# Masks of the products of keys ahead of the split of weights and of y's centring, and the blocks to invert loaded in two transfers

## The chip, the cores and the metric

One core of one Trainium2 chip. The metric is the device time of one execution in microseconds (us); lower is better. The core has TensorE (matrix products, in the rows PE; its weight loads PEld), VectorE (DVE), ScalarE (ACT), GpSimd (POOL) and SyncE (SP, which here issues every DMA). Each runs its own program in order and waits for the others by semaphores.

## The reference

One decoder block on x of 1024 positions by 2048 channels, in float32. A first RMSNorm, one input projection, and then two groups of heads side by side; their gated outputs go through one output projection, are added to x, and a last RMSNorm follows.

```python
h = rmsnorm(x, norm_gain[l])
proj = (h @ w_in[l]).astype(f32)
y_rwkv = rwkv7_group(...)            # 16 heads of 64 channels
y_attn = swa_sink_alibi_group(...)   # 16 query heads, 2 key/value heads, window of 128
x = x + concatenate([y_rwkv, y_attn]) @ w_out[l]
return rmsnorm(x, final_gain)
```

The first group (RWKV-7) is a recurrence over time for each head, `S = S * w + (-(S kk)) b^T + v k^T`, `y = S r`; then y is centred and scaled over the 64 channels of its head (`(y - mean) * rsqrt(var + eps)`), and gated. The second group is attention over a sliding window with a sink and linear position biases.

## The kernel before

**Tiling.** The sequence is taken in two halves of 512 positions, the heads in 8 pairs of 128 channels, so that there are 16 intervals of work, here called pairs 0 to 15 (`INTERVALS`; `i` in the helpers of the recurrence, and `j` in those of the channels). The projections run through everything as a background: weights come in quarters of a tile (128 x 512, 256 KB). For each quarter `gq` SyncE loads `w_raw` (`load_w`, L338), ScalarE rounds it to `w_hi` (`high`, L544), VectorE takes the rest `w_lo = w_raw - w_hi` (`low`, L749; its semaphore is `w_ready`), and TensorE makes 12 matmuls of 128 x 512 of it (`quarter`, L1179). There are 3 buffers of `w_raw` and 5 each of `w_hi` and `w_lo`.

**The order of the work.** All five engines walk over the same loop `for gq in range(QUARTERS)`. Each quarter of about 3 us is given, by hand, pieces of the pairs' work: `current(gq)` yields each pair j with its own quarter number `at = gq - base(j)`. A pair starts each 24 quarters (36 between pairs 7 and 8) and has 38 of them. So `at == 25` of pair j is the same quarter as `at == 1` of pair j + 1, in which `j - 1` stands for the pair whose recurrence is worked on. In each quarter, VectorE takes first `softmax_norm` (at 8), then `low(gq + 4)`, then some x tiles, then `masked` (at 1), then `recurrence` and `channels`, and last `centre` (at 24). ScalarE takes `high(gq + 4)` first. SyncE takes `load_w(gq + 6)` first, which waits for the split of the quarter three before it, since the buffer is shared:

```python
def load_w(gq):
    if gq >= RAW:
        sp.wait_ge(w_ready, gq - RAW + 1)
```

and then the transfers of `recurrence`: at 2 it waits for `a_read` (the masks) and stores four parts of the masked products in `scratch_L` (L378); at 3 it loads them back as `sub_l` (L385), spread over all 128 partitions; at 12 and 13 it brings the inverses back (L389 to L405). Then comes `load_up` (L369).

**The blocks to invert.** The recurrence needs, for each of 128 chunks, the inverse of a triangular matrix of keys. TensorE makes the products at 1 (`products`, L1243, in two halves, each ending in `a_full`); VectorE multiplies them by a mask into `am`, a part of `late` (`masked`, L919, four instructions, two for each half). GpSimd (`inverses`) turns the 32 x 32 diagonal blocks: in step s it reads row s of `sub_l`, in two instructions a step (L500, L502), 31 steps, and a copy (L503). After the way back over DRAM TensorE goes on at 16 with `under` (L1351), which waits for `x_back`.

**What else stands near.** After `products` TensorE makes the decay and learning-rate products of the next pair into banks 2 and 3 (L1205). ScalarE then takes at 26 the sigmoid of the last pair's gate (L619, which waits for `g_ready`, the end of the shift of g on VectorE, L782 and L783), and behind it at 2 the next pair's sigmoid of bank 2 (L596, semaphore `sigma_w`). TensorE's turns at 3 (`turns`, L1164) write bank 2 and wait for `sigma_w`. `centre` (L1025 to L1027) takes the mean out of y; ScalarE squares the result (L669). The sum of squares of r k (`rkr`) is split by L891 at 23 and used by TensorE at 24 (L1226). In the last pair of a half (`last_of_half`: 7 and 15) the tile GA_T is also read at 23.

Of the kernel before, what the change touches and what calls it, by code (L numbers as in the profile page):

```python
# [29 lines left out]
SUB = 32  # L30
SETS = 4
OWN = SUB // SETS
HALF = T // 2
SB = BT // 2
KEYS = BT + SB
# [123 lines left out]
def program(nc, io, scr):  # L159
    with ExitStack() as ctx:  # L160
# [8 lines left out]
        def sem(name):  # L169
# [113 lines left out]

        a_full, a_read = sem("a_full"), sem("a_read")
        t_full, t_read, kkt_full, kkt_read = sem("t_full"), sem("t_read"), sem("kkt_full"), sem("kkt_read")
        l_out, l_in, sub_done, x_out, x_back = (sem("l_out"), sem("l_in"), sem("sub_done"), sem("x_out"),
                                                sem("x_back"))
        s_full, s_read, negmax = sem("s_full"), sem("s_read"), sem("negmax")
        p_ready, p_norm = sem("p_ready"), sem("p_norm")
# [40 lines left out]
        with nc.Block() as block:  # L330
            @block.sync
            def _(sp):
# [38 lines left out]
                def recurrence(i, at):  # L371
                    if at == 2:
                        sp.wait_ge(a_read, 2 * i + 2)
                        blocks = scr["L"].rearrange("(x c m s t) -> x c s m t", x=2, c=2, s=SUB, t=SUB)
                        for x in range(2):
                            for c in range(2):
                                first = us_rows(c).start + SUB * x
                                sp.dma_start(blocks[x, c],  # L378
                                             am[first:first + SUB, :, :, c, 1 - c, SUB * x:SUB * (x + 1)].rearrange(
                                                 "s b h t -> s (b h) t")).then_inc(l_out, 16)  # L380
                    if at == 3:
                        sp.wait_ge(l_out, 4 * 16 * (i + 1))
                        sp.wait_ge(sub_done, i)
                        blocks = scr["L"].rearrange("(p f) -> p f", f=SUB * SUB).unsqueeze(1)
                        sp.dma_start(sub_l[:].rearrange("p s t -> p (s t)"),  # L385
                                     blocks.broadcast_to([PLACES, SETS, SUB * SUB])).then_inc(l_in, 16)
                    if at == 12:
                        sp.wait_ge(sub_done, i + 1)
                        sp.dma_start(scr["X"].rearrange("(p f) -> p f", p=HD), sub_io[0:HD, 0]).then_inc(x_out, 16)  # L389
                        rows = scr["XT"].rearrange("(p j q s) -> q p j s", j=OWN, q=SETS, s=SUB)  # L390
                        for q_ in range(SETS):
                            sp.dma_start(rows[q_], sub_xt[q_::SETS]).then_inc(x_out, 16)  # L392
                    if at == 13:
                        sp.wait_ge(x_out, (1 + SETS) * 16 * (i + 1))
                        columns = scr["X"].rearrange("(c m s j) -> c s m j", c=2, s=SUB, j=OWN)
                        for c in range(2):
                            first = us_rows(c).start
                            sp.dma_start(sub_io[first:first + SUB, 0].rearrange("s (m j) -> s m j", j=OWN), columns[c]
                                         ).then_inc(x_back, 16)
                        sp.wait_ge(u_full, 2 * i)  # L400
                        rows = scr["XT"].rearrange("(x m h t s) -> x h t m s", x=2, h=2, t=SUB, s=SUB)
                        for hh in range(2):
                            for x in range(2):
                                first = HD * hh + SUB * x
                                sp.dma_start(xt[first:first + SUB, :, SUB * x:SUB * (x + 1)], rows[x, hh]  # L405
                                             ).then_inc(x_back, 16)
                    h, n = divmod(i, PAIRS)
                    cols = slice(h * HALF, (h + 1) * HALF)
                    if at == 20:
                        sp.wait_ge(mixa_ready, 2 * i + 2)  # L410
                        sp.dma_start(scr["MIX"][PAIRS + n, :, cols], sa[:]).then_inc(mixa_stored, 16)
                    if at == 35:
                        sp.wait_ge(mix_ready, i + 1)
                        sp.dma_start(scr["MIX"][n, :, cols], ym[:].rearrange("p m t -> p (m t)")
                                     ).then_inc(mix_stored, 16)
# [64 lines left out]
            def _(pool):  # L480
# [7 lines left out]
                def inverses(i):  # L488
                    pool.wait_ge(x_out, (1 + SETS) * 16 * i)
                    if i:  # L490
                        pool.wait_ge(lev_full, 2 * i - 1)
                    pool.wait_ge(ident_landed, 16)
                    then(nc.gpsimd.tensor_copy(sub_io[:, 0], sub_ident[:]))
                    pool.wait_ge(l_in, 16 * (i + 1))
                    for s in range(SUB - 1):
                        below, width = SUB - 1 - s, s // SETS + 1
                        left = sub_l[:, s, s + 1:].unsqueeze(2).broadcast_to([P, below, width])
                        right = sub_x[:, s, 0:width].unsqueeze(1).broadcast_to([P, below, width])
                        t = sub_t[:, 0:below * width].rearrange("p (r c) -> p r c", c=width)
                        then(nc.gpsimd.tensor_tensor(t, left, right, ALU.mult))  # L500
                        rows = sub_x[:, s + 1:, 0:width]
                        then(nc.gpsimd.tensor_tensor(rows, rows, t, ALU.subtract))  # L502
                    then(nc.gpsimd.tensor_copy(sub_xt, sub_x.rearrange("p s j -> p j s")))  # L503
                    pool.sem_inc(sub_done, 1)
# [234 lines left out]
            def _(dve):  # L739
# [86 lines left out]
                def channels(j, at):  # L826
# [42 lines left out]
                    if at == (16 if last_of_half(j) else 20):  # L869
                        dve.wait_ge(kkt_full, j)  # L870
                        then(nc.vector.scalar_tensor_tensor(k, k, p(n, "k_k"), grow, ALU.mult, ALU.mult))
                        for c in range(2):
                            ins = nc.vector.tensor_tensor(
                                qr[:, :, 2 - c], k.rearrange(chunks, b=NB, c=2)[:, :, c],
                                decay[:, :, 0:C].rearrange("p (b c) t -> p b c t", c=2)[:, :, c], ALU.mult)
                        then(ins)
                        dve.sem_inc(kk_read, 1)
                    if at == (23 if last_of_half(j) else 16):
                        read_tile(tile_of(j, GA_T), g)
                        dve.sem_inc(ga_ready, 1)  # L880
# [5 lines left out]
                        evicted(tile_of(j, R_T), h, 4 * n + 2)  # L886
                    if at == (17 if last_of_half(j) else 20):
                        shift(r, p(n, "mu_r"))
                    if at == 23:
                        dve.wait_ge(rkr_high, j + 1)  # L890
                        then(nc.vector.tensor_tensor(kkt_r[:], s1, zs_r[:].bitcast(F32), ALU.subtract))  # L891
                        dve.sem_inc(rkr_split, 1)
                    if at == 19 and j % 4 == 0:
                        between_blocks(j)
                    if at == 21:
# [226 lines left out]
                for gq in range(QUARTERS):  # L1122
                    for j, at in current(gq):
                        if j >= 1 and at == 8:
                            softmax_norm(j - 1, 0)
                    if gq + 4 < QUARTERS:
                        low(gq + 4)
                    for j, at in current(gq):
                        if j >= 1 and at == 18:
                            keys_by_chunk(j - 1)  # L1130
                    cg = chunk_group(gq)
                    if cg:
                        slices(*cg)
                    for j, at in current(gq):
                        if j >= 1 and at == 1:
                            masked(j - 1, 0)
                            masked(j - 1, 1)
                    for j, at in current(gq):
                        if j >= 1:
                            recurrence(j - 1, at)  # L1140
                        if j < INTERVALS:
                            channels(j, at)
                    for j, at in current(gq):
                        if j >= 1 and at == 24:
                            centre(j - 1)
                    prepare(gq)
                    for u in range(2 * KC - 1):
                        if gq == done(OUT0 + u):
                            add(u)
                    if gq == 4 * OUT1 + 7:  # L1150
                        dve.wait_ge(fgain_landed, 16)
                        invert(0)
                    if 0 <= gq - 4 * OUT1 - 8 < KC:
                        scale(0, gq - 4 * OUT1 - 8)
# [400 lines left out]
```

## Time and profile before

| | |
|---|---|
| runs, median of 3 | 1896.99 us (1889.05 to 1900.61) |
| profiled execution | 1890.13 us, its span 1888.4 us |
| granted TensorE clock over the span | 0.993 of full speed (2.4 GHz) |
| TensorE, matmuls | 97% busy |
| VectorE | 66% busy |
| ScalarE | 42% busy |
| GpSimd | 25% busy |
| sixteen DMA engines, queue of SyncE | 36.7% of their time |

A share of busy time is an average over the whole span. TensorE's matmuls are pipelined, so a busy TensorE is not one at its peak, but its idle time is all that a reordering can give back. What a change is worth is read from the waits: who stood for whom, and how long. Times in the rows are microseconds from the start of the span, and `[1.01 <-DMA xt<-scratch_XT]` behind an instruction says that its engine stood idle for 1.01 us before it, until that transfer landed.

### The profile page before, as it was taken

The numbers are of one execution on the slowest core, as the hardware profiler recorded it, in microseconds if no ns is written. First come the engines' busy times: TensorE is split into PE (matmuls) and PEld (weight loads), VectorE is DVE, ScalarE is ACT, GpSimd is POOL, SyncE is SP. The second block draws the span as 40 slices with busy tenths as digits, with TensorE's granted clock in tenths as the row PEclk, the third lists the DMA queues.
The fourth block names the chain that finished last, engine by engine and source line by source line (L and its number), as shares of the span: only waits on it lengthen the run. The fifth ranks groups of instructions, "written<-read, shape, count | busy, mean of one in ns | idle before, by whom it ended". The sixth has DMA issues, their size and how long they took to land.

```text
span 1888.4 us, 38120 instructions
## 1 busy us (share of the span) xinstructions
PE 1840.0 (97%) x15008; PEld 1499.5 (79%) x15008; DVE 1245.9 (66%) x2255; ACT 788.2 (42%) x1578; POOL 466.3 (25%) x1096
## 2 busy tenths in 40 slices
PE   8999999999999999999999999999999999999996
PEld 5878878788888887888788878887877778888885
DVE  5676777677767677667677767676777754355333
ACT  6534444443434345444343434343534543242221
POOL 0005051423324150051423324150505060111110
PEclk9999999999999999999999999999999999999998
DMA  5533332333333336333333333333333543465443
GB/s 180 174 98 96 93 93 83 93 89 93 89 89 98 88 90 175 105 87 85 94 93 90 92 82 96 92 90 87 93 89 100 161 131 101 128 206 173 154 125 123
DMA packets 194962, 207.69 MB, mean 110 GB/s; under 512 B 98272, under 2 KB 101472, under 8 KB 194784
## 3 DMA queue, kind: packets, MB, share of 16 engines
q1 hardware_dynamic: 194784, 205.26, 36.7%
q8 instruction: 118, 1.93, 0.4%
q14 instruction: 60, 0.49, 0.1%
HBM read 183.18 MB, written 22.02 MB: 109 GB/s over the span
## 4 chain that ended last, share of the span: by engine, by line
PE 58%; POOL 16%; DVE 7%; DMA 7%; issue 5%; SPq 4%; ACT 1%; DVEq 0%; POOLq 0%; ACTq 0%
PE psum L1179 48%; POOL sub_io L502 8%; POOL sub_t L500 8%; DMA sub_l<-scratch_L 3%; DVE late L919 2%; DMA scratch_XT<-sub_io 1%; SPq L392 1%; PE psum L1308 1%; DMA xt<-scratch_XT 1%; SPq L405 1%; PE psum L1460 1%; PE psum L1424 1%; DVE w_lo L749 1%; DMA scratch_L<-late 1%; PE psum L1342 1%
## 5 line engine op out<-in xcount | busy, mean ns | idle before, releaser
L1179 PE MATMUL psum<-x_hi,w_hi 128*128 128x512 f32 x2144 | 873.4, 407 | 11.1 <-DVE x_lo L758 7.0
L1179 PE MATMUL psum<-x_hi,w_lo 128*128 128x512 f32 x2144 | 839.8, 392 | 0.0
L1179 PE MATMUL psum<-x_lo,w_hi 128*128 128x512 f32 x2144 | 838.9, 391 | 0.0
L749 DVE TENSOR_TENSOR w_lo<-w_raw,w_hi 128x512 fp32r<-128x512 f32 x536 | 372.0, 695 | 513.5 <-ACT w_hi L544 487.1
L544 ACT ACTIVATE w_hi<-w_raw 128x512 fp32r<-128x512 f32 x536 | 335.4, 629 | 780.8 <-PE psum L1179 685.9
L1179 PEld LDWEIGHTS psum<-x_hi,w_hi 128*128 128x128 f32 x2144 | 403.9, 188 | 111.0 <-issue 14.4
L1179 PEld LDWEIGHTS psum<-x_hi,w_lo 128*128 128x128 f32 x2144 | 403.8, 188 | 88.3
L1179 PEld LDWEIGHTS psum<-x_lo,w_hi 128*128 128x128 f32 x2144 | 404.8, 189 | 79.2 <-issue 3.9
L500 POOL TENSOR_TENSOR sub_t<-sub_l,sub_io 128x60 f32<-128x60 f32 (+24 forms) x496 | 188.3, 380 | 905.1 <-DMA sub_l<-scratch_L 867.4
L502 POOL TENSOR_TENSOR sub_io<-sub_io,sub_t 128x60 f32<-128x60 f32 (+24 forms) x496 | 199.5, 402 | 38.8
L521 POOL TENSOR_TENSOR v<-v,kb 128x512 f32<-128x512 f32 x29 | 38.3, 1321 | 269.1 <-ACT kb L693 268.7
L544 ACT ACTIVATE states<-psum,pc 128x64 f32<-128x64 f32 x112 | 35.0, 312 | 94.1 <-PE psum L1460 94.0
L544 ACT ACTIVATE late<-psum 64x256 f32<-64x256 f32 (+2 forms) x128 | 58.3, 482 | 17.0 <-PE psum L1342 16.3
L1460 PEld LDWEIGHTS psum<-states,score 128*128 128x128 f32 x256 | 47.9, 188 | 12.6 <-ACT states L544 2.0
L624 ACT ACTIVATE score<-score,top 128x192 f32<-128x192 f32 x128 | 56.3, 444 | 0.0
L868 DVE RECIPROCAL work<-work 128x512 f32<-128x512 f32 x16 | 53.6, 3353 | 2.0
L767 DVE TENSOR_TENSOR raw<-psum,rms 128x512 f32<-128x512 f32 x68 | 46.7, 686 | 3.4
L1308 PEld LDWEIGHTS psum<-pt,va 64*64 64x64 f32 (+1 forms) x512 | 34.9, 136 | 13.4 <-issue 11.3
L1460 PE MATMUL psum<-states,score 128*128 128x64 f32 x256 | 42.3, 246 | 0.7 <-ACT states L544 0.5
L919 DVE TENSOR_TENSOR late<-psum,cst 128x512 f32<-128x512 f32 x64 | 41.1, 683 | 2.7 <-DVE late L919 0.5
L1308 PE MATMUL psum<-pt,va 64*64 64x64 f32 (+1 forms) x512 | 41.5, 226 | 0.0
L1308 PE MATMUL psum<-pt,vs 64*64 64x64 f32 (+1 forms) x512 | 41.1, 226 | 0.0
(241 smaller groups left out, 1825.9 us busy)
## 6 DMA issues: line engine op xcount, KB each, us to landing
w_raw<-in_w_in SPq DMA_DIRECT2D x408, 256.0 KB, 2.6
w_raw<-in_w_out SPq DMA_DIRECT2D x128, 256.0 KB, 2.6
sub_l<-scratch_L SPq DMA_DIRECT2D x16, 512.0 KB, 4.7
stage<-in_x_t SPq DMA_DIRECT2D x20, 256.0 KB, 3.3
stage<-scratch_MIX SPq DMA_DIRECT2D x19, 256.0 KB, 4.0
late<-in_x_t SPq DMA_DIRECT2D x16, 256.0 KB, 3.0
scratch_MIX<-sa SPq DMA_DIRECT2D x16, 256.0 KB, 4.3
scratch_MIX<-ym SPq DMA_DIRECT2D x16, 256.0 KB, 3.2
```

The lines of the kernel that those rows point to most:

```text
L500: then(nc.gpsimd.tensor_tensor(t, left, right, ALU.mult))
L502: then(nc.gpsimd.tensor_tensor(rows, rows, t, ALU.subtract))
L521: then(nc.gpsimd.tensor_tensor(c_acc[:], c_acc[:], c_sq[u % 2], ALU.add))
L544: return nc.scalar.activation(dst, src, ACT.Copy, scale=scale)
L624: nc.scalar.activation(prob[:, x], prob[:, x], ACT.Exp, bias=top[:, 1, x:x + 1], accum_out=top[:, 2, x:x + 1])
L749: nc.vector.tensor_tensor(w_lo[gq % SPLIT][:], w_raw[gq % RAW][:], w_hi[gq % SPLIT][:].bitcast(F32), ALU.subtract).then_inc(w_ready, 1)
L767: then(nc.vector.tensor_tensor(dst, psum[:, s % 2], rms[s // H1][:], ALU.mult))
L868: then(nc.vector.reciprocal(grow, grow))
L919: ins = nc.vector.tensor_tensor(am[:, 2 * half:2 * half + 2, hh].rearrange("p b c x t -> p b (c x t)"), psum[:, bank].rearrange("p (b t) - ...
L1179: mm = nc.tensor.matmul(psum[:, s % 2], wt[gq % SPLIT][:, cols], xx[:, c], start=(c == 0 and wt is w_hi and xx is x_hi), stop=(c == KC - 1 ...
L1308: mm = nc.tensor.matmul(psum[head_rows(hh), (6, 2)[rnd], at:at + SB], keys, pt[keys_rows[f][hh], bb, f * P + sub * SB:f * P + (sub + 1) * SB],
L1460: nc.tensor.matmul(psum[:, 6, m * HD:(m + 1) * HD], mt[:, m], states[:, m], start=False, stop=True, skip_group_check=True).then_inc(state_ ...
```

## The change

VectorE's order in a quarter: `masked` (at 1) comes ahead of `low(gq + 4)`. `centre` moves from the end of quarter 24 to quarter 25, which is the same quarter as the next pair's `masked`, behind it and ahead of `low`. The split of rkr (L891) moves, within `channels`, ahead of the read of GA_T. The load of `sub_l` becomes two transfers: rows 0 to 7 of all blocks (128 KB), then rows 8 to 31 (384 KB), each with its own semaphore, and GpSimd waits for the second ahead of step 8. The programs of TensorE and ScalarE are unchanged, and so is all of SyncE's but the one load.

```diff
+ROWS = 8
@@ SyncE, at 3
-                        blocks = scr["L"].rearrange("(p f) -> p f", f=SUB * SUB).unsqueeze(1)
-                        sp.dma_start(sub_l[:].rearrange("p s t -> p (s t)"),
-                                     blocks.broadcast_to([PLACES, SETS, SUB * SUB])).then_inc(l_in, 16)
+                        blocks = scr["L"].rearrange("(p s t) -> p s t", s=SUB, t=SUB)
+                        for rows, landed in ((slice(0, ROWS), l_first), (slice(ROWS, SUB), l_rest)):
+                            part_ = blocks[:, rows].rearrange("p s t -> p (s t)").unsqueeze(1)
+                            sp.dma_start(sub_l[:, rows].rearrange("p s t -> p (s t)"),
+                                         part_.broadcast_to([PLACES, SETS, part_.shape[2]])).then_inc(landed, 16)
@@ GpSimd, inverses
-                    pool.wait_ge(l_in, 16 * (i + 1))
+                    pool.wait_ge(l_first, 16 * (i + 1))
                     for s in range(SUB - 1):
+                        if s == ROWS:
+                            pool.wait_ge(l_rest, 16 * (i + 1))
@@ VectorE, channels
+                    if at == 23:
+                        dve.wait_ge(rkr_high, j + 1)
+                        then(nc.vector.tensor_tensor(kkt_r[:], s1, zs_r[:].bitcast(F32), ALU.subtract))
+                        dve.sem_inc(rkr_split, 1)
                     if at == (23 if last_of_half(j) else 16):
                         read_tile(tile_of(j, GA_T), g)
                         dve.sem_inc(ga_ready, 1)
...
-                    if at == 23:
-                        dve.wait_ge(rkr_high, j + 1)
-                        then(nc.vector.tensor_tensor(kkt_r[:], s1, zs_r[:].bitcast(F32), ALU.subtract))
-                        dve.sem_inc(rkr_split, 1)
@@ VectorE, the loop over quarters
                         if j >= 1 and at == 8:
                             softmax_norm(j - 1, 0)
+                    for j, at in current(gq):
+                        if j >= 1 and at == 1:
+                            masked(j - 1, 0)
+                            masked(j - 1, 1)
+                    for j, at in current(gq):
+                        if j >= 1 and at == 25:
+                            centre(j - 1)
                     if gq + 4 < QUARTERS:
                         low(gq + 4)
...
-                    for j, at in current(gq):
-                        if j >= 1 and at == 1:
-                            masked(j - 1, 0)
-                            masked(j - 1, 1)
                     for j, at in current(gq):
                         if j >= 1:
                             recurrence(j - 1, at)
                         if j < INTERVALS:
                             channels(j, at)
-                    for j, at in current(gq):
-                        if j >= 1 and at == 24:
-                            centre(j - 1)
```

## Rows read from the trace of the kernel before

**Rows 1.** The page, part 1: engine, busy us (share of the span) x instructions.

```profile
PE 1840.0 (97%) x15008; PEld 1499.5 (79%) x15008; DVE 1245.9 (66%) x2255; ACT 788.2 (42%) x1578; POOL 466.3 (25%) x1096
```

**Rows 2.** Waits of TensorE, whole span: total us, times, longest us.

```profile
PE psum L1351 <- DMA xt<-scratch_XT: 15.4, 13, 2.6
...
PE psum L1226 <- DVEq L892: 4.4, 3, 4.0
```

**Rows 3.** Timeline of TensorE: first and last of 13 stops at L1351.

```profile
275.53 0.39 PE L1351 MATMUL psum<-sub_io,late 32*32 32x32 f32 x13 [1.01 <-DMA xt<-scratch_XT]
...
1552.15 0.36 PE L1351 MATMUL psum<-sub_io,late 32*32 32x32 f32 x12 [2.59 <-DMA xt<-scratch_XT]
```

**Rows 4.** Chain that ended last, pair 3: start, us, what.

```profile
405.98 1.64 DMA scratch_L<-late
407.64 4.64 DMA sub_l<-scratch_L
...
419.67 0.31 POOL sub_t L500
...
441.46 0.67 POOL sub_io L503
```

**Rows 5.** Timeline of all engines, pair 3: start, us, engine, line, instruction.

```profile
399.28 2.06 PE L1243 MATMUL psum<-qr,kb 64*128 64x128 f32 x32
...
399.46 0.68 DVE L1025 TENSOR_REDUCE stat<-ym 128x8 f32<-128x512 f32 x1
...
401.22 0.69 DVE L749 TENSOR_TENSOR w_lo<-w_raw,w_hi 128x512 fp32r<-128x512 f32 x1
401.82 2.72 DVE L919 TENSOR_TENSOR late<-psum,cst 128x512 f32<-128x512 f32 x4
401.93 0.33 SPq L338 DMA_DIRECT2D w_raw<-in_w_in  x1
404.63 1.81 SPq L378 DMA_DIRECT2D scratch_L<-late  x4
404.69 0.69 DVE L782 TENSOR_TENSOR work<-raw 128x512 f32<-128x512 f32 x1
405.42 0.75 DVE L783 SCALAR_TENSOR_TENSOR work<-work,par,raw 128x512 f32<-128x512 f32 x1
406.26 0.63 ACT L619 ACTIVATE work<-work 128x512 f32<-128x512 f32 x1 [0.37 <-DVEq L908]
...
406.80 0.67 ACT L596 ACTIVATE work<-psum,par 128x512 f32<-128x512 f32 x1
...
407.72 1.03 PE L1164 MATMUL psum<-cst,kb 128*128 128x128 f32 x8
```

**Rows 6.** Timeline, pair 0: the turns wait for ScalarE.

```profile
143.33 0.67 ACT L596 ACTIVATE work<-psum,par 128x512 f32<-128x512 f32 x1
...
144.14 0.52 PE L1164 MATMUL psum<-cst,kb 128*128 128x128 f32 x3 [0.67 <-ACT work L596]
```

**Rows 7.** Timeline, pair 3: VectorE's first softmax, and TensorE's use of it.

```profile
426.11 1.17 DVE L958 TENSOR_SCALAR score<-score,part 128x192 f32<-128x192 f32 x4
...
428.01 0.82 PE L1164 MATMUL psum<-cst,score 128*128 128x128 f32 x6
```

**Rows 8.** DMA issues: count, KB each, median us from issue to landing.

```profile
w_raw<-in_w_in SPq DMA_DIRECT2D x408, 256.0 KB, 2.6
...
lora_up<-in_lora_up SPq DMA_DIRECT2D x16, 64.0 KB, 4.1
...
sub_ident<-in_sub_ident SPq DMA_DIRECT2D x1, 128.0 KB, 2.3
```

**Rows 9.** The line L385 (`sub_l`), all 16 of its transfers.

```profile
DMA to landing us min/median/max: 3.8/4.7/5.3
```

**Rows 10.** Timeline of VectorE, pair 15, whose products start at 1497.96.

```profile
1500.82 0.69 DVE L1025 TENSOR_REDUCE stat<-ym 128x8 f32<-128x512 f32 x1
...
1508.48 0.69 DVE L749 TENSOR_TENSOR w_lo<-w_raw,w_hi 128x512 fp32r<-128x512 f32 x1
```

More of the change, by code:

```diff
@@ L285, in program @@
         t_full, t_read, kkt_full, kkt_read = sem("t_full"), sem("t_read"), sem("kkt_full"), sem("kkt_read")
-        l_out, l_in, sub_done, x_out, x_back = (sem("l_out"), sem("l_in"), sem("sub_done"), sem("x_out"),
+        l_out, l_first, l_rest, sub_done, x_out, x_back = (sem("l_out"), sem("l_first"), sem("l_rest"), sem("sub_done"), sem("x_out"),
                                                 sem("x_back"))
```

## The prediction

> **What bounds the kernel now.** I read the page first. TensorE is busy 97% of the span [rows 1], so the most that any reordering can give back is its idle time. The waits of TensorE tell where that is [rows 2]: 15.4 us in 13 stops at the first matmul of L1351 (`under`), which waits for the transfer that brings the inverted blocks home; 4.4 us at L1226, of which 4.0 us is one stop; and 0.67 us in one pair at L1164, for ScalarE's L596 [rows 6]. Nothing else that this change touches is of size. The 13 stops at L1351 (first and last in [rows 3]; in the order of the pairs they are 1.01, 1.44, 0.45, 0.86, 0.69, 0.70, then 1.26, 2.34, 0.36, 1.13, 0.74, 1.78, 2.59 us, for pairs 1 to 6, 8, and 10 to 15) are small beside the chain that ends in them. The chain of waits of one pair [rows 4] goes: masks on VectorE, four stores of blocks to DRAM whose last lands 1.64 us after its issue, the load of `sub_l` (4.64 us, to 412.28), GpSimd until 442.13 (some 30 us), and the way back. Its length from the products' first matmul to L1351 is fixed, so a chain that is shorter by d gives each pair the smaller of d and its stop, and a chain that is longer by d costs d.
>
> The timeline around the products [rows 5] shows the place of the edit. The products (L1243) run from 399.28 to 401.34. VectorE is behind at that moment and does centre (L1025, from 399.46), the split `low` (L749, 401.22 to 401.91), then four masks (L919, 401.82 to 404.54), then the shift of g (L782, L783, to 406.17). The other engines hang on it without slack: SyncE issues one weight load (L338) at 401.93, that is 0.02 us after the split, then the stores (L378) at 404.63, 0.09 us after the masks; ScalarE starts the sigmoid of g (L619) 0.09 us after the shift, then L596, which ends at 407.47; and TensorE starts the turns (L1164), which wait for L596, at 407.72.
>
> **The masks, moved ahead of centre and split.** Their work is unchanged. They can't start at 399.46, since they need the first half of the products. That half is done in the middle of L1243, about 400.37 (estimate: half of 2.06 us). So they run from about 400.45 to 403.17 (2.72 us), 1.37 us sooner than now; VectorE idles almost 1 us ahead of them, which it doesn't now. Centre then starts at 403.32 (a drain of 0.15 us, as between masks and L782), the split 1.76 us later (as 399.46 to 401.22) at 405.08, ending at 405.77 instead of 401.91.
>
> What queues behind the split? In SyncE's program, the quarter with the stores begins with `load_w(gq + 6)`, which waits for `w_ready` of gq + 4, the very split that is now behind masks and centre. SyncE is in order. So the weight load goes out at 405.79, takes 0.33 us to issue, and the stores begin at about 406.17: not 1.37 us sooner but 1.54 us later than 404.63. The early masks buy nothing on this chain, and the chain pays 1.54 us. The weight load itself, 3.9 us late, I cost at nothing: in the loops it is issued two quarters ahead of ScalarE's use of it, and lands 2.6 us after its issue [rows 8]. If that cover were gone, its 3.9 us would stand in the way of a quarter, in 13 pairs.
>
> **ScalarE and the turns.** The shift of g starts 0.60 us after the split's start (as L919 does now), at 405.68, and ends 1.48 us later at 407.16. L619 starts at 407.25, L596 0.54 us later at 407.79, and ends at 408.46. The pair in which the turns now stop longest for L596 shows the latency [rows 6]: L596 ends at 144.00, the matmul starts at 144.14. So the turns start at 408.60 instead of 407.72: TensorE stands for 0.88 us, a new stop in each of the pairs that have centre beside masks and a next pair's sigmoid, which are 13 (1 to 6 and 8 to 14). Behind it, ScalarE's evictions and exponentials come about 1 us late, and so does VectorE's first softmax; its last multiply ends at 427.28 now, and the matmul that needs it starts at 428.01 [rows 7]. With TensorE itself 0.88 us later, the slack of 0.73 us becomes 1.6 us, more than 1 us of delay: nothing added.
>
> A stop at the turns delays TensorE, not GpSimd, and so is paid out of the stop at L1351 where that one is longer.
>
> **The load of sub_l in two parts.** Now it lands 3.8 to 5.3 us after issue, 4.7 us at the median [rows 9]. GpSimd needs only the first 8 rows, 128 KB, to start. Bounds: nothing gained (the first part lands at 4.7 us too, because it queues behind the weight load, as a 64 KB load of `lora_up` issued right behind `sub_l` takes 4.1 us [rows 8]); and 3.1 us gained (it lands in the 1.6 us of a 32 KB store). I take the one row of 128 KB, `sub_ident`, 2.3 us: gained 2.4 us. The weight load ahead takes 2.6 us and will be issued about 1.1 us ahead, so it is mostly past. The second part is issued some 0.55 us later; GpSimd reaches step 8 at 419.67, 7.4 us after it could begin [rows 4], so its wait at step 8 is covered; without that cover it would cost what the part is late. One more issue on SyncE, 0.5 us, delays only `load_up`.
>
> The Trainium skill (DMA: Bandwidth & Descriptors, Anatomy of one DMA — SWDGE (gpsimd) path) gives a transfer about 2.0 us fixed and bytes over 436 GB/s, and so an estimate of 2.3 us for 128 KB and 3.2 us for 512 KB. By it the split would gain only 0.9 us, and the sum would be 7.5 us slower. The trace agrees with it on 128 KB (2.3 us) and not on 512 KB (4.7 us).
>
> **The split of rkr (L891) ahead of the read of GA_T.** It changes order only in pairs 7 and 15 (`last_of_half`). L1226 stops for it there for 0.17 and 0.16 us, which can't give more than 0.3 us. The large stop of 4.0 us is in pair 0, where nothing moves.
>
> **The sum.** Chain: 1.54 − 2.4 = −0.86 us. TensorE's own way: +0.88 us. A pair changes by the larger of (0.88 − its stop) and −0.86: for pairs 1 to 6 −0.13, −0.56, +0.43, +0.02, +0.19, +0.18; for 8 to 14 −0.38, +0.88 (pair 9 has no stop), −0.86, +0.52, −0.25, +0.14, −0.86. Together −0.7 us. Pair 15 is apart [rows 10]: VectorE reaches centre at 1500.82, 2.9 us after its products' start, so the masks lose nothing waiting; no sigmoid of a next pair follows; and the load of `sub_l` already waits for a later split (L749, 1508.48 to 1509.17), which moves by some 0.1 us. It gives 2.3 us of its 2.59. Pairs 0 and 7 have no stop and nothing to lose. With 0.3 us for rkr: −3.3 us. The profiled execution took 1890.1 us, so 1886.8; it lies 6.9 us below the median of the runs shown, 1897.0, and on that median the forecast is 1893.7.
>
> **Rivals.**
> A, the stops go away: if the turns don't stop anew (the new order lets ScalarE keep its time), each pair gives the smaller of 0.86 and its stop, 9.0 us, with pair 15 and rkr 11.6 us: 1885.4. If SyncE isn't held either, all of 15.4 + 0.3 us: 1881.3. For it speaks that the masks are ready sooner; against it L338 at 401.93 and L596's 0.25 us of slack. Chance 0.13.
> B, slower: the first part lands hardly sooner, and the late stores decide. It decides from a gain of under 1.55 us; with none, 13 pairs × 1.54 us − 0.3 = +19.8 us: 1916.8. For it speaks the `lora_up` row; against it `sub_ident`. Chance 0.10.
> B2, the transfer is mostly fixed cost, and a quarter of the bytes saves only 0.9 us (3.8 us, the shortest landing of `sub_l`): the chain is 0.64 us longer, twelve pairs × 0.64 + 0.88 − 0.8 (pair 15) − 0.3 = +7.5 us: 1904.5. Chance 0.09, as the median of 4.7 us speaks against so small a part for bytes. The rule of the Trainium skill above (DMA: Bandwidth & Descriptors) is of this kind.
> C, ScalarE's delay is handed on to the softmax or the evictions, and TensorE stops once more, 0.5 us in each of 13 pairs: up to +6.5 − 3.3 = +3.2 us, 1900.2. Against it the slack in [rows 7]. Chance 0.10.
> The forecast itself, −9 to +3 us, has 0.58.
>
> **How the numbers follow.** About 1% (19 us) is what a measurement of this kernel can tell from no change. Faster by more than that would need more than all stops at L1351: 0.04. Slower by more needs B with almost no gain, or B with C: 0.09. The rest, 0.87. The three runs before lie between 1889 and 1901, so the median of few runs is uncertain by some 5 us; with A on one side and B2 on the other, 1884 to 1906. The likeliest case's own range is 1889 to 1898.
>
> **What would show it.** VectorE idle ahead of L919 until the products are done, about 0.9 us in 13 pairs; L378 about 6.9 us after the start of L1243 (now 5.35); L619 about 8.0 us after it (now 6.98); a wait of TensorE at L1164 for L596 of about 11 us in total; L1351's waits down from 15.4 us to about 1 us; `sub_l`'s first part landing in 2.3 us; GpSimd's first multiply about 12.3 us after L1243 (now 13.1). If L378 stands at 4.0, SyncE's hold was misread; if GpSimd starts later than now, B; if L1164 shows no wait, A. Wrong would be above all a clearly shorter or longer first landing, since each 0.5 us of it moves seven or more pairs.

## Result: 0.37% slower

| | median | lowest to highest | runs |
|---|---|---|---|
| before | 1892.78 us | 1888.41 to 1902.30 | 20 |
| changed | 1899.87 us | 1895.48 to 1907.11 | 20 |

The ratio is 1.0037, with an interval of 1.0025 to 1.0049: 7.1 us slower, where 3.3 us faster was forecast. Measured again later (the last experiment below) it was 1.0036 (1.0022 to 1.0051).

Line numbers in the changed kernel are 1 to 5 higher: 339 for the weight load, 379 for the stores, 388 for `sub_l`, 505 and 507 for GpSimd's steps, 601 and 624 for the sigmoids, 754 for the split, 836 for VectorE's scan (831 before), 924 for the masks, 1030 for centre, 1169 for the turns, 1248 for the products, 1356 for `under`.

The waits of TensorE in the changed kernel (total us, times, longest us), which answer to [rows 2]:

```profile
PE psum L1169 <- ACT work L601: 10.8, 15, 0.8
PE psum L1356 <- DMA xt<-scratch_XT: 9.9, 12, 1.8
...
PE psum L1231 <- DVEq L886: 4.0, 1, 4.0
PE psum L1368 <- DVEq L1000: 1.6, 2, 1.2
...
PE psum L1248 <- DVEq L1066: 0.9, 1, 0.9
```

The new stop at the turns is there, 10.8 us. But the stops at `under` fell only from 15.4 to 9.9 us: the chain behind them did not get shorter.

The timeline of pair 3, which answers to [rows 5]; its products start at 400.02:

```profile
400.02 2.06 PE L1248 MATMUL psum<-qr,kb 64*128 64x128 f32 x32
...
401.23 2.72 DVE L924 TENSOR_TENSOR late<-psum,cst 128x512 f32<-128x512 f32 x4 [0.94 <-PE psum L1248]
...
404.10 0.69 DVE L1030 TENSOR_REDUCE stat<-ym 128x8 f32<-128x512 f32 x1
...
405.86 0.69 DVE L754 TENSOR_TENSOR w_lo<-w_raw,w_hi 128x512 fp32r<-128x512 f32 x1
...
406.58 0.33 SPq L339 DMA_DIRECT2D w_raw<-in_w_in  x1
406.95 1.92 SPq L379 DMA_DIRECT2D scratch_L<-late  x4
...
408.03 0.63 ACT L624 ACTIVATE work<-work 128x512 f32<-128x512 f32 x1 [1.07 <-DVEq L913]
...
408.57 0.67 ACT L601 ACTIVATE work<-psum,par 128x512 f32<-128x512 f32 x1
...
409.38 1.06 PE L1169 MATMUL psum<-cst,kb 128*128 128x128 f32 x8 [0.77 <-ACT work L601]
```

The masks wait 0.94 us for the products. The split ends at 406.55, the weight load goes out 0.03 us later and the stores behind it, 6.93 us after the products' start (5.35 before), though the masks were done at 403.95, which is 3.93 us after it. The sigmoid of g starts at 8.01 us (6.98 before), and the turns stop for 0.77 us.

### The profile page after: what moved, and what is told of

Its sections match the earlier page's. It is cut to its first block, busy times and chain, and to the rows that moved or that the text cites. A ratio compares the mean times of both kernels' runs of the same rounds, so it can differ in the third digit from the quotient of the medians.

```text
span 1900.8 us, 38152 instructions
## 1 busy us (share of the span) xinstructions
PE 1844.7 (97%) x15008; PEld 1500.5 (79%) x15008; DVE 1246.7 (66%) x2255; ACT 785.8 (41%) x1578; POOL 474.0 (25%) x1096
## 4 chain that ended last, share of the span: by engine, by line
PE 61%; POOL 17%; DVE 7%; DMA 6%; SPq 4%; issue 4%; ACT 1%; DVEq 0%; POOLq 0%; ACTq 0%
PE psum L1184 49%; POOL sub_io L507 8%; POOL sub_t L505 8%; DVE late L924 2%; DMA sub_l<-scratch_L 2%; PE psum L1313 1%; SPq L395 1%; DMA scratch_XT<-sub_io 1%; PE psum L1465 1%; DMA scratch_L<-late 1%; DMA xt<-scratch_XT 1%; SPq L408 1%; PE psum L1248 1%; PE psum L1429 1%; DVE w_lo L754 1%
## 5 line engine op out<-in xcount | busy, mean ns | idle before, releaser
L674 ACT ACTIVATE zs<-ym 128x512 f32<-128x512 f32 x16 | 10.1, 633 | 77.6 <-DVEq L1034 77.6
```

## What GpSimd meets when it begins

All distances below are in us from the start of a pair's products (only the fifth column is a length), averaged over the 13 pairs of the forecast (1 to 6 and 8 to 14), each read from the timeline of one profiled execution.

| run | stores | load of sub_l | GpSimd starts | its steps and copy | ends | `under` starts |
|---|---|---|---|---|---|---|
| before | 5.37 | 8.40 | 13.13 | 30.03 | 43.16 | 53.13 |
| changed | 6.93 | 10.18 | 13.02 | 30.69 | 43.71 | 53.69 |
| two loads only | 5.38 | 8.39 | 11.64 | 30.97 | 42.61 | 52.70 |
| moves only | 6.94 | 10.20 | 14.30 | 29.93 | 44.23 | 54.29 |
| centring back | 5.90 | 9.19 | 11.99 | 30.58 | 42.57 | 52.62 |
| stores first | 4.02 | 7.03 | 10.08 | 31.14 | 41.22 | 53.02 |
| both | 4.75 | 7.76 | 10.62 | 30.66 | 41.28 | 52.06 |
| scan first | 6.94 | 10.20 | 13.03 | 29.33 | 42.36 | 53.01 |
| two loads, scan first | 5.38 | 8.39 | 11.76 | 29.66 | 41.42 | 52.12 |

The chain to `under` grew by 0.56 us in the changed kernel, instead of shrinking by 0.86 us. One part of that is in the column that the forecast took as fixed: GpSimd's own time. Its first instructions in pair 1 of the kernel before, with VectorE's scan ahead of them (start us, us):

```profile
234.46 1.23 DVE L831 TENSOR_TENSOR_SCAN work<-keep,work 128x512 f32<-128x512 uint8 x1
```

```profile
235.78 0.24 POOL L500 TENSOR_TENSOR sub_t<-sub_l,sub_io 128x31 f32<-128x31 f32 x1 [47.26 <-DMA sub_l<-scratch_L]
236.10 0.28 POOL L502 TENSOR_TENSOR sub_io<-sub_io,sub_t 128x31 f32<-128x31 f32 x1
```

The same in the changed kernel:

```profile
235.78 1.26 DVE L836 TENSOR_TENSOR_SCAN work<-keep,work 128x512 f32<-128x512 uint8 x1
```

```profile
235.73 0.24 POOL L505 TENSOR_TENSOR sub_t<-sub_l,sub_io 128x31 f32<-128x31 f32 x1 [46.86 <-DMA sub_l<-scratch_L]
236.04 1.07 POOL L507 TENSOR_TENSOR sub_io<-sub_io,sub_t 128x31 f32<-128x31 f32 x1
```

Before, the scan ended at 235.69, just ahead of GpSimd. The shift of ScalarE's work that the forecast put at about 1 us carries the scan with it (it waits for `sigma_w`, and behind a scaling of y that waits for ScalarE too), and now it runs from 235.78 to 237.04. GpSimd's second instruction takes 1.07 us for what took 0.28 us, and ends at 237.11, with the scan (in pairs 3, 6, 10 and 11 its first instruction is caught instead, with 0.83 to 1.24 us for 0.24 us). GpSimd can start sooner, but it doesn't get on.

## Experiments

The theory after the result had four parts: (1) SyncE's weight load, behind the split, holds the stores; (2) centre ahead of the split makes the stop at the turns; (3) the first part of `sub_l` saves less than 2.4 us; (4) GpSimd doesn't proceed beside VectorE's scan. The rivals were that the two transfers bring nothing, that the turns alone cost the time, and that the second transfer, landing beside GpSimd's first steps, slows them.

**Two loads only.** The kernel before with the load in two parts.

```diff
-                        sp.dma_start(sub_l[:].rearrange("p s t -> p (s t)"),
-                                     blocks.broadcast_to([PLACES, SETS, SUB * SUB])).then_inc(l_in, 16)
+                        for rows, landed in ((slice(0, ROWS), l_first), (slice(ROWS, SUB), l_rest)):
...
+                        if s == ROWS:
+                            pool.wait_ge(l_rest, 16 * (i + 1))
```

> The kernel before, with the load of sub_l in two parts and nothing else changed. Theory: the changed kernel gains at this place what it loses at two others (SyncE's hold, the turns). Alone, the split starts GpSimd about 1.9 us sooner, 11.2 us after the products' start instead of 13.1, with no new stop at the turns; the 13 stops of L1351 (15.4 us) shrink to under 2 us and the kernel is 12 to 14 us faster (ratio about 0.993). GpSimd's inverses took 30.6 us in the changed kernel and 29.9 before: if the second transfer that lands beside them is the cause, they take 30.6 us here too, and the gain is nearer 11 us. Rival: two transfers cost as much as they bring, GpSimd starts at 12.5 us or later and the kernel is within 0.2% of before.

Measured: 1884.12 us against 1894.37 us of the kernel before, ratio 0.9945 (0.9925 to 0.9966), 10 us faster. GpSimd starts 1.5 us sooner, but its steps and copy take 0.9 us longer, so that it ends 0.55 us sooner on average, and 7.1 us of stops stay at `under`. In eleven of the 13 pairs it ended between 42.55 and 42.58 us, whether it had started at 11.21 or at 11.89 us. What holds it, in pair 1:

```profile
235.29 0.69 DVE L1075 TENSOR_TENSOR ym<-ym,stat 128x512 f32<-128x512 f32 x1
...
236.13 1.23 DVE L836 TENSOR_TENSOR_SCAN work<-keep,work 128x512 f32<-128x512 uint8 x1
```

```profile
235.29 0.79 POOL L505 TENSOR_TENSOR sub_t<-sub_l,sub_io 128x31 f32<-128x31 f32 x1 [45.10 <-DMA sub_l<-scratch_L]
236.16 1.26 POOL L507 TENSOR_TENSOR sub_io<-sub_io,sub_t 128x31 f32<-128x31 f32 x1
```

The split of the load is worth having; most of what it brings is then waited off behind the scan. The scan isn't alone in this: the scaling of y ahead of it (L1075, which has two inputs in SBUF too) held GpSimd's first instruction for 0.79 us instead of 0.24 us. The first expectation, 12 to 14 us, was too high, as were the stops that it left (under 2 us), and its second reading (30.6 us because of the second transfer, 11 us) had the right size: the next two runs tell which of the two causes is at work.

**Moves only.** The changed kernel with `sub_l` in one transfer again.

> The changed kernel with sub_l loaded in one transfer again; masks, centre and rkr stay moved. Theory (SyncE's weight load, queued ahead of the stores, waits for the split that is now behind masks and centre): stores at 6.9 us after the products' start, GpSimd starts at 14.6 to 15 us, TensorE stops 0.77 us at the turns in 13 pairs and the rest at L1356; 20 to 24 us slower than before (ratio about 1.011). If GpSimd's inverses take 30.6 us here, it is VectorE's new order that slows them, and the loss is nearer 28 us. Rival (the stores' time doesn't matter, the turns alone cost): 8 to 10 us slower, as the changed kernel.

Measured: 1911.04 us, ratio 1.009 (1.0069 to 1.011), 16.7 us slower. The stores stand at 6.94 us, so (1) holds without the split, and the rival of the turns alone (8 to 10 us) falls. GpSimd takes 29.93 us: VectorE's order does not slow it by itself, since at 14.30 us it starts behind the scan. GpSimd starts 4.1 us after the load's issue instead of 4.7 us, and the loss was under the 20 us expected. What changed around the load is that the weight load now goes 2.0 us ahead of it, where it went 0.6 us ahead before; that this is the cause was not tested by itself. The kernel before, pair 3:

```profile
407.03 0.35 SPq L338 DMA_DIRECT2D w_raw<-in_w_in  x1
407.64 0.54 SPq L385 DMA_DIRECT2D sub_l<-scratch_L  x1
```

The run with the moves only, the same pair:

```profile
409.07 1.91 SPq L379 DMA_DIRECT2D scratch_L<-late  x4
411.02 0.46 SPq L339 DMA_DIRECT2D w_raw<-in_w_in  x1
413.00 0.54 SPq L386 DMA_DIRECT2D sub_l<-scratch_L  x1
```

**Centring back.** The changed kernel with `centre` at the end of quarter 24.

```diff
-                        if j >= 1 and at == 25:
-                            centre(j - 1)
...
+                        if j >= 1 and at == 24:
+                            centre(j - 1)
```

> The changed kernel with y's centring back at the end of quarter 24; masks still ahead of the weight split. Theory: VectorE then does centre while the products are made, masks from 1.9 to 4.7 us, the split to 5.5 us, the stores go out at 5.9 us (6.9 in the changed kernel, 5.35 before), the shift of g ends as before and the stop at the turns is gone (10.8 us to under 1 us). Together with the two loads GpSimd starts about 12 us after the products; 8 to 10 us faster than before (ratio about 0.995). Rival (masks ahead of the split are what costs at the turns, not centre): 0.7 us stops at the turns stay.

Measured: 1886.63 us, ratio 0.9961 (0.9946 to 0.9975), 7.7 us faster than before, just under what was expected. The stores go out at 5.90 us and the waits of TensorE at the turns are as before the change (total us, times, longest us):

```profile
PE psum L1169 <- ACT work L601: 0.8, 2, 0.7
```

So (2) holds, and masks ahead of the split cost nothing at the turns.

**Both: centring back, and SyncE's stores and load ahead of its weight load.** The edit of SyncE (the one of `centre` is shown above):

```diff
                 for gq in range(QUARTERS):
+                    for j, at in current(gq):
+                        if j >= 1 and at in (2, 3):
+                            recurrence(j - 1, at)
                     if gq + 6 < QUARTERS:
                         load_w(gq + 6)
...
-                        if j >= 1:
+                        if j >= 1 and at not in (2, 3):
                             recurrence(j - 1, at)
```

> As the run with the centring back, and SyncE's transfers of quarters 2 and 3 go ahead of the weight load of their quarter. Theory: stores at 4.7 us after the products' start, right behind the masks, sub_l's load at 7.7 us, GpSimd starts at 10.6 us instead of 13.1, the chain is 1.9 to 2.5 us shorter and takes all stops of L1351 but a few tenths; no stop at the turns; 13 to 17 us faster than before (ratio about 0.992). Rival (the hold of SyncE is not what sets the stores): stores at 5.9 us, as with the centring back alone.

Measured: 1879.27 us, ratio 0.9919 (0.9899 to 0.9939), 15.1 us faster. The stores leave at 4.75 us, 0.08 us behind the masks, so it was the weight load that held them. TensorE never stops at `under`, and pairs 1 to 5 and 8 to 13 each take 87.13 to 87.17 us: the length of TensorE's own work.

**Stores first, VectorE's order as changed.** The same edit of SyncE on the changed kernel.

> The changed kernel, with SyncE's transfers of quarters 2 and 3 ahead of the weight load of their quarter; VectorE's order stays as changed. Theory: stores at 4.0 us after the products' start instead of 6.9, sub_l's load at about 7.1 us, GpSimd starts near 10 us, all stops of TensorE at L1356 are gone; the stops at the turns (0.77 us in 13 pairs) stay, as they come from the shift of g behind centre and split. So TensorE's own way sets the time: 13 x 0.84 us more than before against 15.4 us of stops less, 2 to 5 us faster than before. Rival (the stores are held by something else, or the turns' stop hangs on SyncE): stores stay at 6.9 us, or the stops at the turns go.

Measured: 1889.92 us, ratio 0.9989 (0.9977 to 1.0001), 2.8 us less than before, at the low end of what was expected, and with an interval that reaches no change. The waits of TensorE (total us, times, longest us) hold no line for `under`:

```profile
PE psum L1172 <- ACT work L604: 10.9, 15, 0.8
```

The same pairs take 88.1 us each here, against 87.14 us in the run with both: about 1 us in each is what centre ahead of the split costs by the turns once the chain is out of the way. In the changed kernel most of it is hidden behind the stops at `under`.

**Scan first.** The changed kernel with VectorE's scan ahead of the scaling of y, nothing else (`summed_up` is the scan, taken out of `channels` at 3).

```diff
+                    for j, at in current(gq):
+                        if j < INTERVALS and at == 3:
+                            summed_up(j)
                     for j, at in current(gq):
                         if j >= 1:
                             recurrence(j - 1, at)
```

> The changed kernel with one instruction of VectorE moved: the scan (1.23 us) goes ahead of the scaling of y in its quarter, so that it runs near 10.4 us after the products' start and not at 13.0 us, when GpSimd begins. Theory: GpSimd's second instruction took 1.07 us there instead of 0.27 us, because it doesn't proceed beside the scan; with the scan gone it takes 0.3 us, GpSimd's inverses 29.8 to 30.0 us instead of 30.6, and end 0.5 us sooner; the stops of L1356 fall from 9.9 us to 4 to 6 us, 4 to 5 us faster than the changed kernel, 2 to 4 us slower than before. Rival (the 0.8 us comes from the second transfer landing beside GpSimd's first steps): the second instruction stays near 1 us.

Measured: 1892.66 us, ratio to the kernel before 0.9996 (0.9986 to 1.0006), where the changed kernel has 1.0037. The move of one instruction gives back the whole 7 us; 4 to 5 us had been expected. Pair 1:

```profile
233.60 1.22 DVE L918 TENSOR_TENSOR_SCAN work<-keep,work 128x512 f32<-128x512 uint8 x1
```

```profile
235.63 0.36 POOL L505 TENSOR_TENSOR sub_t<-sub_l,sub_io 128x31 f32<-128x31 f32 x1 [46.88 <-DMA sub_l<-scratch_L]
236.07 0.27 POOL L507 TENSOR_TENSOR sub_io<-sub_io,sub_t 128x31 f32<-128x31 f32 x1
```

GpSimd starts where it did in the changed kernel (13.03 us), with the second transfer landing beside it, and its second instruction takes 0.27 us. That rules out the rival of the second transfer, and shows (4): its work takes 29.33 instead of 30.69 us. Of these 1.36 us some 0.8 us stand at the first two instructions; the rest is spread over later steps, which meet other instructions of VectorE than they did, and no run separates it. All stops at `under` went but one of 2.7 us in pair 15.

**Two loads and the scan first**, on the kernel before: nothing of the moves.

> The kernel before with the load of sub_l in two parts and VectorE's scan ahead of the scaling of y; masks, centre and rkr where they were. Theory: the scan runs near 10.1 to 11.3 us after the products' start and no longer beside GpSimd's first steps (there it held them until 13.3 us however early they began, so that GpSimd's end stood at 42.55 us for starts from 11.2 to 12.0). GpSimd then ends at 41.2 to 41.9 us, all stops of TensorE at L1351 but a few tenths are gone, no stop at the turns: each pair takes 87.14 us, 13 to 16 us faster than before, as the run with both holds gone. Rival (something else sets GpSimd's end): 42.55 us stays, and 10 us faster.

Measured: 1881.48 us against 1897.88 us, ratio 0.991 (0.9896 to 0.9923), 16 us faster. GpSimd ends at 41.42 us on average; the 42.55 us are gone.

**Rkr only.** The kernel before with L891 ahead of the read of GA_T.

> The kernel before with the split of rkr alone moved ahead of the read of GA_T. It acts in pairs 7 and 15 only. The two stops of 0.17 us at L1226 go; in pair 15 the sigmoid behind the later read of GA_T delays ScalarE by 0.7 us and y's first sum by as much, and TensorE stops about 0.9 us at the products' second half, as in the changed kernel. Together within 1 us of before, not to be told from it. Rival: a clear change either way.

Measured: 1894.13 us against 1892.73 us, ratio 1.0004 (0.9991 to 1.0017): nothing that can be told. The stop at the products of pair 15 is in its waits as in those of the changed kernel (0.9 us). In the changed kernel the sigmoid behind the later read waits (start us, us):

```profile
1507.98 0.63 ACT L621 ACTIVATE work<-work 128x512 f32<-128x512 f32 x1 [0.72 <-DVEq L889]
```

**First part of two rows only** (32 KB), on the kernel before; a single run.

> The kernel before with the load of sub_l in two parts, but only 2 rows (32 KB) in the first and 30 (480 KB) in the second. If a landing goes by bytes, the first lands about 2.0 to 2.3 us after issue (128 KB took 2.7 to 3.1 us, 32 KB stores 1.6 us); if a fixed cost and the weight load ahead set it, it stays at 2.7 us or more. GpSimd has only about 1.5 us of work before step 2 and then waits for the second part, which lands 4.2 to 4.6 us after its issue at 8.9 us, so that step 2 starts at about 13.3 us and nearly nothing is left of the gain: 0 to 3 us faster than before.

Measured: 1881.03 us in one run, against 1892.73 us (1887.31 to 1900.22 in 29 runs). The profile page has the two parts' landing:

```profile
sub_l<-scratch_L SPq DMA_DIRECT2D x16, 480.0 KB, 3.8
...
sub_l<-scratch_L SPq DMA_DIRECT2D x16, 32.0 KB, 2.4
```

This expectation failed on the gain: 0 to 3 us was expected, and the run was 12 us below the median of before. The second part landed in 3.8 us, not 4.2 to 4.6, and was there when step 2 wanted it. One run doesn't tell whether 2 rows are better than 8.

**Both, without the move of rkr.**

> The run with the centring back and SyncE's transfers first, with the split of rkr back behind the read of GA_T. The stop of 0.9 us at the products of pair 15 goes, two of 0.17 us at L1226 come back: 0.5 us faster than with it, which can't be told; 13 to 16 us faster than before.

Measured: 1880.33 us against 1897.88 us, ratio 0.9903 (0.9889 to 0.9917). With both (0.9919) and with two loads and the scan first (0.991) it is the fastest of the kernels measured more than once, and the three can't be told from each other; all three beat both the kernel before and the changed one.

**The changed kernel again.**

> The changed kernel once more, on the chip of the two others, to compare with: 5 to 9 us slower than before, GpSimd's end at 43.5 us in most pairs (its second instruction stands beside the scan), 10 to 11 us of stops at the turns and 9 to 11 us at L1356.

Measured: 1903.87 us, ratio 1.0036 (1.0022 to 1.0051). The stops at the turns were 10.9 us as expected; those at L1356 were 16.7 us, more than the 9 to 11 us expected. GpSimd ended at 43.86 us on average, and the way back over DRAM took 10.3 us instead of 10.0. So the stops at `under` vary from one execution of the same kernel to another by several us.

## Why the forecast was wrong, step by step

**The masks and SyncE's hold** were right: VectorE idle for 0.94 us (about 0.9 forecast), the stores at 6.93 us (about 6.9). **The turns** were right: 0.77 us instead of 0.88 us per pair, 10.8 us in all (about 11). So was the rule that a pair takes the larger of the two: in the run with stores first TensorE's own way alone set the time.

**The load in two parts: the term of 2.4 us was too large.** The transfer began at 10.18 us, 1.78 us later than before, not 1.54 us. GpSimd started 2.84 us after its issue, 4.73 us before: 1.9 us gained. Of these, 0.6 us came with the moves alone (4.10 us in the run with the moves only), and 1.3 us from the size. The one row of 128 KB, `sub_ident` at 2.3 us [rows 8], was from the start of the program; here 128 KB took 2.7 us by the profile page. The Trainium skill (DMA: Bandwidth & Descriptors, Anatomy of one DMA — SWDGE (gpsimd) path) would have a saving of 0.9 us by its estimate, which is for transfers that GpSimd issues, where SyncE issues them here. With equal surroundings the runs show 1.3 us (moves only against changed) and 1.5 us (before against two loads only), between that and mine.

**The term that was missing: GpSimd's own time**, +0.66 us. The forecast had called the chain's length fixed from the products to `under`, whatever the new order. It followed ScalarE's delay to the softmax and stopped there; it did not ask what VectorE would be doing when GpSimd begins. The Trainium skill (GPSIMD Engine Reference, Key points) says that GpSimd shares its SBUF interfaces with VectorE and contends with instructions that have two SBUF inputs; the scan has two, and the trace agrees: 1.07 us beside it, 0.27 us without it. With these two terms the waits at `under` came to 9.9 us, not the 1 us of the forecast's list of signs, and GpSimd's first multiply to 13.0 us, not 12.3 us.

So the chain is 1.78 − 1.89 + 0.66 = +0.55 us instead of −0.86 us. By the forecast's own rule 12 pairs then pay 0.55 us, and pair 9 the 0.84 us of TensorE's way (pair 5 of the changed kernel, without a stop at `under`, takes 88.12 us, pair 9 before 87.28 us): +7.4 us.

**Pair 15 and the edit of rkr.** The forecast had −2.3 us here; `under` came 53.94 us after the products' start, instead of 54.19 us: −0.25 us. The reading that SyncE's hold moves by only 0.1 us in this pair was wrong: the stores left at 9.54 us instead of 8.04 us, most of it through rkr. With rkr alone moved they left at 8.98 us, TensorE stopped for 0.9 us inside the products, and `under` came at 55.23 us. So the edit of rkr was wrong in sign too, by its waits (two stops of 0.17 us less, one of 0.9 us more); in the time of the kernel nothing of it can be told.

**How well the account closes.** These terms give some 7 us, and 7.1 us were measured, but the agreement is closer than the profiles allow. In the first profile of the changed kernel the 13 pairs together took 12.9 us longer than in the profile of before: 7.2 us of this lies ahead of `under` (the sum above), 5.6 us behind it. In the second profile it was 15.9 us, 13.5 us ahead and 2.4 us behind. What lies behind `under` is in no term of the forecast. The largest part is in pair 14 of the first profile, where TensorE stops for VectorE:

```profile
1474.26 0.45 PE L1368 MATMUL psum<-xt,ym 32*32 32x32 f32 x32 [1.18 <-DVEq L1000]
...
1476.84 0.79 PE L1184 MATMUL psum<-x_hi,w_hi 128*128 128x512 f32 x1 [2.13 <-DVEq L776]
```

The longer of the two, of 1.5 to 2.1 us, is in pair 14 of every other profile as well, and only the profile of before lacks it, so it can't be put down to the change. It also means that the stop at `under` in pair 14 wasn't there to be won: the pair took 92.65 us with 1.34 us of it (centring back) and 92.65 us with none (both). The forecast had counted 0.86 us there.

Rival B2 gave almost the measured time (+7.5 us), but not for its reason: the first part gained more than the 0.9 us that it allowed. The price of the scan made up the rest, so that it came near the number was luck. B's point of decision, a gain of 1.55 us, was passed by the transfer (1.9 us), but the chain became longer all the same.

The clock doesn't carry the difference: the median granted clock was 0.993 over the 20 runs of the changed kernel, and 0.991 over 16 runs of the kernel before (0.992 and 0.9905 where both were measured side by side). But it makes a stop dearer in one execution than in another, as the last part shows.

## What to carry to other kernels

When an edit moves an instruction on an in-order engine, list what each other engine has queued behind that instruction's semaphore: here a weight load that nobody was short of held the stores that everybody waited for, and to put the urgent transfers first was worth 7 us (with both against centring back alone) to 9 us (stores first against the changed kernel, by their ratios). When a wait of GpSimd is shortened, look at what VectorE runs at the new starting time: an instruction with two SBUF inputs beside GpSimd's start took away what a faster transfer had brought. And an edit that shortens one chain is worth only as much as the other chain leaves, so price both before adding up, and look behind each stop for the next one.

## What the runs showed of the hardware

**GpSimd beside a scan.** A subtraction of 31 elements took 0.27 to 0.28 us alone and 1.07 to 1.28 us beside VectorE's scan, and ended with it. Therefore GpSimd's later steps stood at the same time in pair after pair, whatever its start had been. The same shows beside other instructions of VectorE. The kernel before, pair 1, the split of weights (two inputs in SBUF) and a subtraction of 16 elements, which took 0.24 us for 24 elements one step earlier:

```profile
263.73 0.69 DVE L749 TENSOR_TENSOR w_lo<-w_raw,w_hi 128x512 fp32r<-128x512 f32 x1 [2.71 <-ACT w_hi L544]
```

```profile
263.81 0.69 POOL L502 TENSOR_TENSOR sub_io<-sub_io,sub_t 128x16 f32<-128x16 f32 x1
```

So VectorE holds GpSimd at more places than beside the scan; no run took these out.

**The clock after a stop.** In pair 12 of the changed kernel's second profile TensorE stopped for 2.08 us at `under`, ahead of 1296.3. Stretches of that profile (us, busy us of each engine, granted clock, DMA share, GB/s):

```profile
1290.00:1293.00 3.00, 3.00 (x15) 2.48 (x14) 0.99 (x2) 0.56 (x1) 0.12 (x1) 1.00 0.71 115
1293.00:1296.00 3.00, 1.25 (x6) 0.71 (x4) 2.04 (x3) 0.07 (x1) 0.00 (x0) 1.00 0.63 68
1296.00:1299.00 3.00, 2.66 (x39) 2.17 (x40) 0.18 (x1) 0.63 (x1) 0.40 (x1) 0.81 0.64 243
1299.00:1302.00 3.00, 3.00 (x40) 2.08 (x39) 1.60 (x4) 0.36 (x1) 0.00 (x0) 0.62 0.30 87
1302.00:1305.00 3.00, 3.00 (x18) 2.24 (x20) 2.02 (x6) 2.23 (x4) 0.00 (x0) 1.00 0.25 81
```

Behind the stop, and the small products of `under` that follow it, the clock fell from 2.4 to 1.2 GHz for a part of the next 6 us, and this pair took 91.8 us. Pair 1 of the same profile took 88.3 us with a stop of 0.1 us; 2.0 us of the difference is the longer stop, and some 1.5 us the clock. The same happened in pairs 2 and 3 of that profile, after stops of 1.76 and 1.56 us (91.5 and 91.3 us), in pair 4 of the first profile, after 1.44 us (91.2 us), and in pair 10 of the kernel before, after 2.34 us (91.1 us); but not in pair 2 of the kernel before, after 1.44 us (88.7 us), nor in pair 14 of the second profile, after 1.98 us. Where it fell, the pair was 1.5 to 1.6 us longer than its stop explains. In two stretches from about the same place of pair 10 in the run with both, where TensorE didn't stop, the clock stayed:

```profile
1101.00:1104.00 3.00, 3.00 (x44) 2.20 (x43) 1.49 (x3) 0.62 (x1) 0.40 (x1) 1.00 0.84 254
1104.00:1107.00 3.00, 3.00 (x44) 2.25 (x43) 2.04 (x5) 0.92 (x3) 0.00 (x0) 1.00 0.38 107
```

So a stop can cost some 1.6 us beyond its own length. That fits the spread of the runs: 1886 to 1899 us for 16 runs of the kernel before, 1876.6 to 1881.0 us for the six with both. That it explains all of the spread wasn't tested.
